# The second feed-forward layer by seven half-size products a slice

## The chip, the cores and the metric

The kernel runs on one core of a Trainium2 chip. The metric is the device time of one execution in microseconds. Before the change it is 1483.28 us, the median of 3 runs (1483.11 to 1483.89). A profile of one further execution is read beside it; every row below comes from that execution.

Engines: TensorE (PE: matmuls; PEld: its weight loads), VectorE (DVE), ScalarE (ACT), GpSimd (POOL) and SyncE (SP, which issues loads).

## What is computed

Two transformer blocks over 512 rows of 1024 features, in fp32. The change touches the last part of the second block alone:

```
h = rms_norm_2(x, norm_mlp[l])
x = x + jnp.square(jax.nn.relu(h @ w_ff1[l])) @ w_ff2[l]
return rms_norm_2(x, norm_final)
```

`w_ff1` is 1024 x 4096, `w_ff2` 4096 x 1024. Products have to keep the precision of fp32.

## The kernel before

All engines run programs of their own, ordered by semaphores that are written out by hand. A product in fp32 precision is made of three matmuls: each operand is split into a rounded part ("hi", fp32r) and the remainder ("lo"), and hi x hi, hi x lo and lo x hi are summed in PSUM. A matmul takes a 128x128 block as weights and streams 512 columns.

Weights come as "pairs": 256 rows x 512 columns, two blocks of 128 partitions, 512 KB. SP loads a pair into one of four slots of `raw` (`load`, L514) once TensorE has used the pair that was there (`pair_used`); ScalarE rounds it to `w_hi` (`part_hi`, L1566); GpSimd subtracts and writes `w_lo` (`split`, L677). `w_lo` lies where `raw` lay. TensorE waits for `hi_made` and `lo_made` of each pair.

The feed-forward part works in eight slices of 512 hidden features. The first layer of a slice (`ff_up`, L1519) is a "strip": four pairs, 96 matmuls into four of the eight PSUM banks, features on the partitions. VectorE's `hidden` (L2843) empties it with relu and the row scale and squares it (L2852); ScalarE writes the rounded square `ys_hi` (L2175) and VectorE its remainder `ys_lo` (L2855). The second layer multiplies these 512 rows x 512 features by the slice's 512 x 1024 part of `w_ff2`: two strips of two pairs, 48 matmuls each, rows on the partitions, and VectorE adds each strip from PSUM to x (`add_strip`, L2686), which is kept in `proj[:, :, XRES:XRES+1024]`.

TensorE's order is skewed by one slice: in `ff_step` (L1538) the first layer of slice t+1 comes ahead of the second layer of slice t. VectorE, ScalarE and GpSimd follow in the same order, SP in the order of pairs. The very last strip (`last_strip`, L1522) is done row tile by row tile, so that the final norm of one tile runs beside the matmuls of the next. Ahead of the first slice x is turned (transposed) in TensorE and split into `xt_hi` and `xt_lo`; `r_rows`, the row scale, is spread and turned beside the first strip. `gfin` is the final gain, scaled by one VectorE instruction (L2866) after the first `hidden`.

## Time and profile before

| | us |
|---|---|
| median of 3 runs | 1483.28 |
| lowest, highest | 1483.11, 1483.89 |
| span of the profiled execution | 1481.3 |
| TensorE busy | 1446.9 (98%) |
| VectorE busy | 653.3 (44%) |
| ScalarE busy | 620.0 (42%) |
| GpSimd busy | 651.7 (44%) |

The span goes from the first to the last instruction of the profiled execution. Matmuls overlap in a pipeline, so a busy TensorE may still have matmuls further apart than they could be; the distance between their starts says more than their duration. The feed-forward part fills the span from about 1124 us on. A row's idle time is that of the engine just before the instruction, and the name behind the arrow is what ended it. Idle time of an engine that nobody waits for costs nothing.

### The profile page before, as it was taken

To read this page: it belongs to the slowest core of one execution; us is meant where nothing else is said; L and a number is where in the kernel's file an instruction comes from. 1 tells how busy PE (TensorE), PEld (TensorE's weight loads), DVE (VectorE), ACT (ScalarE), POOL (GpSimd) and SP (SyncE) were. 2 spreads that over 40 slices of the span, in tenths; PEclk is the share of its full clock that TensorE was granted. 3 is DMA by queue.
4 is the path that set the end of the run, shared out by engine and by line. 5 is a ranking of instruction groups with operands and counts; after the bars stand their busy time and mean duration, and the time that the engine had idled before them with its cause. 6 is when DMAs were issued, how large, how long until landed. Compare 5 with 4: busy or idle time off the path is not lost.

```text
span 1481.3 us, 20850 instructions
## 1 busy us (share of the span) xinstructions
PE 1446.9 (98%) x7825; PEld 1212.5 (82%) x7825; DVE 653.3 (44%) x1388; ACT 620.0 (42%) x1128; POOL 651.7 (44%) x451
## 2 busy tenths in 40 slices
PE   8999999989989999999999999999999999999998
PEld 7888888768778888899997777888888888888886
DVE  4436959456563131421244777752222422233233
ACT  5443644567563222343235477762324222222223
POOL 4433645344443444434342365644444444444442
PEclk9999999999999999999999999999999999999999
DMA  6222433203002332446432200004222222223222
GB/s 204 81 81 82 153 94 92 61 7 100 29 1 72 100 93 93 156 126 194 128 89 72 72 16 2 2 13 163 96 100 86 100 100 95 90 99 99 99 96 89
DMA packets 73050, 130.44 MB, mean 88 GB/s; under 512 B 5816, under 2 KB 29955, under 8 KB 72963
## 3 DMA queue, kind: packets, MB, share of 16 engines
q1 hardware_dynamic: 71682, 126.04, 26.8%
q10 hardware_dynamic: 1280, 3.22, 0.6%
q8 instruction: 57, 0.93, 0.3%
q14 instruction: 31, 0.25, 0.1%
HBM read 125.05 MB, written 4.19 MB: 87 GB/s over the span
## 4 chain that ended last, share of the span: by engine, by line
PE 94%; DVE 2%; ACT 2%; issue 1%; POOL 1%; DMA 0%; POOLq 0%; SPq 0%; DVEq 0%; ACTq 0%
PE bank L887 74%; PE bank L1118 4%; PE bank L1126 4%; PE bank L949 3%; PE bank L816 3%; PE bank L847 1%; PE bank L951 1%; PE bank L1534 1%; PE bank L1362 0%; PE bank L1069 0%; DVE prob_t L2496 0%; DMA proj<-in_x 0%; DVE q_parts L2380 0%; POOL w_lo L680 0%; PE bank L1015 0%
## 5 line engine op out<-in xcount | busy, mean ns | idle before, releaser
L680 POOL TENSOR_TENSOR w_lo<-raw,w_hi 128x1024 fp32r<-128x1024 f32 (+3 forms) x217 | 508.0, 2343 | 671.2 <-ACT w_hi L1569 671.1
L1569 ACT ACTIVATE w_hi<-raw 128x1024 fp32r<-128x1024 f32 (+3 forms) x221 | 225.6, 1022 | 610.0 <-DMA raw<-in_w_ff 254.6
L887 PE MATMUL bank<-w_hi,xt_hi 128*128 128x484 f32 (+2 forms) x632 | 236.0, 373 | 0.0
L887 PE MATMUL bank<-w_hi,xt_lo 128*128 128x484 f32 (+2 forms) x632 | 233.8, 370 | 0.0
L887 PE MATMUL bank<-w_lo,xt_hi 128*128 128x484 f32 (+2 forms) x632 | 233.7, 370 | 0.0
L887 PE MATMUL bank<-xt_hi,w_hi 128*128 128x512 f32 x560 | 221.2, 395 | 0.0
L887 PE MATMUL bank<-xt_hi,w_lo 128*128 128x512 f32 x560 | 218.2, 390 | 0.0
L887 PE MATMUL bank<-xt_lo,w_hi 128*128 128x512 f32 x560 | 218.0, 389 | 0.0
L887 PEld LDWEIGHTS bank<-w_hi,xt_lo 128*128 128x128 f32 x632 | 118.6, 188 | 14.6
L887 PEld LDWEIGHTS bank<-w_hi,xt_hi 128*128 128x128 f32 x632 | 118.7, 188 | 14.5 <-issue 0.4
L887 PEld LDWEIGHTS bank<-w_lo,xt_hi 128*128 128x128 f32 x632 | 118.7, 188 | 13.8
L887 PEld LDWEIGHTS bank<-xt_hi,w_hi 128*128 128x128 f32 x560 | 105.2, 188 | 23.3 <-issue 2.2
L887 PEld LDWEIGHTS bank<-xt_hi,w_lo 128*128 128x128 f32 x560 | 105.1, 188 | 22.1
L887 PEld LDWEIGHTS bank<-xt_lo,w_hi 128*128 128x128 f32 x560 | 105.2, 188 | 21.5 <-issue 0.5
L887 PE MATMUL bank<-w_hi,ys_hi 128*128 128x512 f32 x240 | 93.4, 389 | 0.0
L887 PE MATMUL bank<-w_lo,ys_hi 128*128 128x512 f32 x240 | 93.4, 389 | 0.0
L887 PE MATMUL bank<-w_hi,ys_lo 128*128 128x512 f32 x240 | 93.4, 389 | 0.0
L2849 DVE SCALAR_TENSOR_TENSOR proj<-bank,r_rows 128x512 f32<-128x512 f32 x32 | 19.9, 683 | 140.3 <-PE bank L887 140.3
L1833 ACT ACTIVATE sc<-sc,negmax 128x512 f32<-128x512 f32 (+3 forms) x104 | 58.8, 567 | 24.7 <-DVE negmax L2472 24.7
L2691 DVE TENSOR_TENSOR proj<-proj,bank 128x512 f32<-128x512 f32 x56 | 34.7, 682 | 69.4 <-PE bank L887 69.4
L816 PE MATMUL bank<-cst,proj 128*128 128x128 f32 (+2 forms) x368 | 50.6, 280 | 7.7 <-DMA proj<-in_x 4.9
L816 PEld LDWEIGHTS bank<-cst,proj 128*128 128x128 f32 (+2 forms) x368 | 43.6, 141 | 13.8 <-DMA cst<-cst_d 4.1
(386 smaller groups left out, 2383.3 us busy)
## 6 DMA issues: line engine op xcount, KB each, us to landing
raw<-in_w_ff SPq DMA_DIRECT2D x64, 512.0 KB, 3.5
raw<-in_w_in SPq DMA_DIRECT2D x40, 512.0 KB, 3.5
raw<-in_w_in SPq DMA_DIRECT2D x40, 484.0 KB, 3.4
raw<-in_w_in SPq DMA_DIRECT2D x24, 392.0 KB, 3.3
raw<-in_w_out SPq DMA_DIRECT2D x16, 512.0 KB, 3.5
raw<-in_w_branch SPq DMA_DIRECT2D x12, 512.0 KB, 3.7
raw<-in_w_mem_kv SPq DMA_DIRECT2D x8, 512.0 KB, 3.6
raw<-in_w_proj_nsa SPq DMA_DIRECT2D x8, 512.0 KB, 3.4
```

Of the source, the lines that this page charges most:

```text
L680: pool.tensor_tensor(w_lo[:, slot, 0:halves, 0:width], raw[:, slot, 0:halves, 0:width], w_hi[:, slot, 0:halves, 0:width].bitcast(F32), ALU ...
L816: ins = pe.transpose(b[0:m, o:o + k], src, ident[0:k, 0:k])
L847: ins = pe.matmul(bank[strip_banks(s)][b][:], lhs, rhs, start=False, stop=kk == 1 and j == 2)
L887: ins = pe.matmul(o, lhs, rhs, start=st and j == 0, stop=en and j == 2)
L949: ins = pe.matmul(o, w["q"], w["k"], start=True, stop=w["k_lo"] is None)
L951: ins = pe.matmul(o, w["q"], w["k_lo"], start=False, stop=True)
L1118: ins = pe.transpose(bank[TURN_BANK + u % 2][0:n, t * P:(t + 1) * P], src[:, t * P:t * P + n], ident)
L1126: ins = pe.matmul(bank[4 + w["pas"] % 2][w["rows"], w["cols"]], w["v"][t], src[0:n, t * P:(t + 1) * P], start=w["start"] and t == 0, stop= ...
L1569: act.activation(w_hi[:, slot, 0:halves, 0:width], raw[:, slot, 0:halves, 0:width], ACT.Copy)\
L1833: act.activation(v, v, ACT.Exp, scale=-1.0, bias=negmax[:, u % SC:u % SC + 1], accum_out=sums[:, u % SC:u % SC + 1]).then_inc(sem["exps"], 1)
L2691: ins = dve.tensor_tensor(v, v, banks[t][:], ALU.add)
L2849: ins = dve.scalar_tensor_tensor(relu[:, m, :], banks[m][:], 0.0, r_rows[:], ALU.max, ALU.mult)
```

## The change

Seven of the eight slices take another algorithm for the second layer; the first layer stays. The slice's activations (512 x 512) are seen as 2 x 2 quarters a11, a12, a21, a22 of 256 x 256, and the slice's weights as 2 x 2 quarters b11, b12, b21, b22 of 256 x 512. Four sums of a-quarters and four differences of b-quarters (one of them in place of b12) are made, and seven products of 256 x 256 by 256 x 512 are summed to give what eight gave.

- TensorE: `product` is 2 x 2 x 3 = 12 matmuls into two banks; `seven_products` orders them 6, 1, 7, 5, 4, 2, 3. It waits for all three `h_hi` and `h_lo` of the slice ahead of the first, for the item (`item_hi`, `item_lo`) ahead of each, and for banks emptied by VectorE. The next slice's strip waits until six of the seven products are added.
- VectorE: four half sums (512 columns for each partition), four quarter sums or differences (1024), three remainders of rows (`rows_lo`: 1024, 512, 2048), then `hidden` of the next slice, then adding the seven products from PSUM, with the square between the third and the fourth. Products 2, 3, 4, 5 go to one quarter of x each; 1, 6 and 7 are kept in `part_sums` and joined to x by five instructions of 1024 columns after the seventh slice.
- ScalarE: `rows_hi` (1024, 512, 2048 columns) and `items_hi` (seven of 1024), then the four pairs of the first layer.
- GpSimd: `items_lo` (seven of 1024), then the four `w_lo` of the first layer. Before it had eight `w_lo` a slice.
- SP: the quarters don't pass the ring of four slots; each has its place and is loaded when the product that reads it last is done. Ahead of the first of them SP waits for all of `xt_hi` and `xt_lo`, as they lie where earlier data lay, and it loads them ahead of the second strip's pairs.
- The eighth slice keeps two strips. Its parts lie in the place of `xt_hi` and `xt_lo`, and its remainder is made after the seventh slice's last product is added.

The core of the diff:

```diff
+PRODUCTS = (6, 1, 7, 5, 4, 2, 3)
+ITEMS = (1, 6, 7, 5, 4, 2, 3)
+ITEM_AFTER = {1: 1, 6: 4, 7: 2, 5: 3, 4: 4, 2: 4, 3: 3}
+RAW_FREE = {"b11": 1, "b12": 7, "b21": 2, "b22": 3}
...
+            def ff2_quarters(f):
+                for n, (name, q, s) in enumerate((("b11", 0, 0), ("b12", 0, 1), ("b21", 1, 0), ("b22", 1, 1))):
+                    if not isinstance(f, int):
+                        sp.wait_ge(sem["product_done"], f * 7 + (PRODUCTS.index(RAW_FREE[name]) - 6))
+                    src = pairs_of(w_ff2_2[0], 0, 0)[f * 2 + q]
+                    sp.dma_start(quarter[name][:], src[:, :, S * s:S * s + S]).then_inc(sem[f"quarter_in{n}"], 16)
...
             ff1_weights(0, PAIR_FF)
-            with sp.Fori(1, 8) as f:
-                ff1_weights(f, f * 8 + (PAIR_FF - 4))
-                ff2_weights(f - 1, f * 8 + PAIR_FF)
-            ff2_weights(7, PAIR_FF + 60)
+            sp.wait_ge(sem["xt_hi"], 24)
+            sp.wait_ge(sem["xt_lo"], 24)
+            ff2_quarters(0)
+            ff1_weights(1, PAIR_FF + 4)
+            with sp.Fori(1, 7) as f:
+                ff1_weights(f + 1, f * 4 + (PAIR_FF + 4))
+                ff2_quarters(f)
...
+            def items_lo(i, t):
+                for n, m in enumerate(ITEMS):
+                    pool.wait_ge(sem["item_hi"], at(i, lambda j: 7 * t(j) + n + 1))
+                    pool.wait_ge(sem["t_made"], at(i, lambda j: 4 * t(j) + ITEM_AFTER[m]))
+                    pool.tensor_tensor(item_lo[m][:], quarter[item_of[m]][:], item_hi[m][:].bitcast(F32), ALU.subtract)\
+                        .then_inc(sem["item_lo"], 1)
...
+            ff1_lo(0, lambda j: PAIR_FF + 4)
+            items_lo(0, lambda j: 0)
+            ff1_lo(0, lambda j: PAIR_FF + 8)
+            with pool.Fori(1, 7) as i:
+                items_lo(i, lambda j: j)
+                ff1_lo(i, lambda j: PAIR_FF + 8 + 4 * j)
...
+            def product(m, banks, first):
+                (a_hi, a_lo), b_hi, b_lo = rows_of[m], item_hi[m], item_lo[m]
+                for kt in range(2):
+                    for u in range(2):
+                        c = slice(u * P, u * P + P)
+                        for j, (lhs, rhs) in enumerate(((a_hi[:, kt, c], b_hi[:, kt, :]), (a_hi[:, kt, c], b_lo[:, kt, :]),
+                                                        (a_lo[:, kt, c], b_hi[:, kt, :]))):
+                            ins = pe.matmul(bank[banks + u][:], lhs, rhs, start=first and kt == 0 and j == 0,
+                                            stop=kt == 1 and j == 2, skip_group_check=True)
+                ins.then_inc(sem["product_done"], 1)
+            def seven_products(i, parity, t):
+                def taken(n):
+                    pe.wait_ge(sem["product_added"], at(i, lambda j: 7 * t(j) + n))
+                pe.wait_ge(sem["h_hi"], at(i, lambda j: 3 * t(j) + 3))
+                pe.wait_ge(sem["h_lo"], at(i, lambda j: 3 * t(j) + 3))
+                two, one, three = 4 * parity, 4 * parity + 2, 4 - 4 * parity
+                for m in PRODUCTS:
+                    n = ITEMS.index(m)
+                    pe.wait_ge(sem["item_hi"], at(i, lambda j: 7 * t(j) + n + 1))
+                    pe.wait_ge(sem["item_lo"], at(i, lambda j: 7 * t(j) + n + 1))
+                    if m == 6:
+                        if not isinstance(i, int):
+                            taken(0)
+                        product(6, two, True)
+                    elif m == 1:
+                        product(1, one, True)
+                    elif m == 7:
+                        taken(1)
+                        product(7, two, False)
+                    elif m == 5:
+                        pe.wait_ge(sem["emptied_d"], at(i, lambda j: strips_emptied("D", STRIP_FF + 1 + t(j))))
+                        product(5, three, True)
+                    elif m == 4:
+                        taken(3)
+                        product(4, two, False)
+                    elif m == 2:
+                        taken(2)
+                        product(2, one, False)
+                    else:
+                        taken(4)
+                        product(3, three, False)
...
+            pe.wait_ge(sem["h_hi"], 22)
+            pe.wait_ge(sem["h_lo"], 22)
+            pe.wait_ge(sem["product_added"], 48)
+            strip(0, lambda j: STRIP_LAST, lambda j: PAIR_LAST, 2, h_last, S, False)
+            pe.wait_ge(sem["product_added"], 49)
+            last_strip(STRIP_LAST + 1, PAIR_LAST + 2)
...
+            def rows_hi(i, t):
+                act.wait_ge(sem["sq_out"], at(i, lambda j: t(j) + 1))
+                if not isinstance(i, int):
+                    act.wait_ge(sem["product_done"], at(i, lambda j: 7 * t(j)))
+                act.activation(a1_hi[:], h_raw[:, :, 0:256], ACT.Copy).then_inc(sem["h_hi"], 1)
+                act.activation(a22_hi[:], h_raw[:, 2:4, 256:512], ACT.Copy).then_inc(sem["h_hi"], 1)
+                act.wait_ge(sem["h_summed"], at(i, lambda j: t(j) + 1))
+                act.activation(s_hi[:], h_sums[:], ACT.Copy).then_inc(sem["h_hi"], 1)
+            def items_hi(i, t):
+                for m in ITEMS:
+                    name = item_of[m]
+                    if name in ("b11", "b21", "b22"):
+                        act.wait_ge(sem[{"b11": "quarter_in0", "b21": "quarter_in2", "b22": "quarter_in3"}[name]],
+                                    at(i, lambda j: 16 * t(j) + 16))
+                    else:
+                        act.wait_ge(sem["t_made"], at(i, lambda j: 4 * t(j) + ("t1", "b12", "t2", "t4").index(name) + 1))
+                    act.activation(item_hi[m][:], quarter[name][:], ACT.Copy).then_inc(sem["item_hi"], 1)
+            def ff_step(i, t):
+                rows_hi(i, t)
+                items_hi(i, t)
+                his(i, lambda j: PAIR_FF + 8 + 4 * t(j))
...
+            act.wait_ge(sem["sq_out"], 8)
+            act.wait_ge(sem["pair_used"], PAIR_LAST)
+            act.activation(h_last[0], h_raw, ACT.Copy).then_inc(sem["h_hi"], 1)
...
+            def hidden(i, f):
+                banks = strip_wait(i, lambda j: STRIP_FF + f(j))
+                wait(dve, sem["h_hi"], at(i, lambda j: 3 * f(j)))
+                wait(dve, sem["h_lo"], at(i, lambda j: 3 * f(j)))
                 for m in range(4):
-                    ins = dve.scalar_tensor_tensor(relu[:, m, :], banks[m][:], 0.0, r_rows[:], ALU.max, ALU.mult)
+                    ins = dve.scalar_tensor_tensor(h_raw[:, m, :], banks[m][:], 0.0, r_rows[:], ALU.max, ALU.mult)
                 ins.then_inc(sem["emptied_d"], 1)
-                dve.wait_ge(sem["emptied_d"], at(i, lambda j: strips_emptied("D", s(j))))
-                dve.tensor_tensor(square, relu, relu, ALU.mult).then_inc(sem["sq_out"], 1)
-                dve.wait_ge(sem["sq_out"], at(i, lambda j: f(j) + 1))
-                dve.wait_ge(sem["h_hi"], at(i, lambda j: f(j) + 1))
-                dve.tensor_tensor(ys[parity][1][:], square, ys[parity][0][:].bitcast(F32), ALU.subtract)\
-                   .then_inc(sem["h_lo"], 1)
+            def square(i, f):
+                dve.wait_ge(sem["emptied_d"], at(i, lambda j: strips_emptied("D", STRIP_FF + f(j))))
+                dve.tensor_tensor(h_raw, h_raw, h_raw, ALU.mult).then_inc(sem["sq_out"], 1)
+            def rows_lo(i, t):
+                dve.wait_ge(sem["h_hi"], at(i, lambda j: 3 * t(j) + 1))
+                dve.tensor_tensor(a1_lo[:], h_raw[:, :, 0:256], a1_hi[:].bitcast(F32), ALU.subtract).then_inc(sem["h_lo"], 1)
+                dve.wait_ge(sem["h_hi"], at(i, lambda j: 3 * t(j) + 2))
+                dve.tensor_tensor(a22_lo[:], a22, a22_hi[:].bitcast(F32), ALU.subtract).then_inc(sem["h_lo"], 1)
+                dve.wait_ge(sem["h_hi"], at(i, lambda j: 3 * t(j) + 3))
+                dve.tensor_tensor(s_lo[:], h_sums[:], s_hi[:].bitcast(F32), ALU.subtract).then_inc(sem["h_lo"], 1)
+            def add_product(i, t, m, banks):
+                dve.wait_ge(sem["product_done"], at(i, lambda j: 7 * t(j) + PRODUCTS.index(m) + 1))
+                for u in range(2):
+                    o = {2: proj[:, u, XRES:XRES + S], 3: proj[:, u, XRES + S:XRES + D],
+                         4: proj[:, 2 + u, XRES:XRES + S], 5: proj[:, 2 + u, XRES + S:XRES + D]}.get(m)
+                    z = {1: 0, 6: 1, 7: 2}.get(m)
+                    if o is not None:
+                        ins = dve.tensor_tensor(o, o, bank[banks + u][:], ALU.add)
+                    elif isinstance(i, int):
+                        ins = dve.tensor_copy(part_sums[z][:, u, :], bank[banks + u][:])
+                    else:
+                        ins = dve.tensor_tensor(part_sums[z][:, u, :], part_sums[z][:, u, :], bank[banks + u][:], ALU.add)
+                ins.then_inc(sem["product_added"], 1)
...
+                t1, t2, t4 = quarter["t1"][:], quarter["t2"][:], quarter["t4"][:]
+                b11, b12, b21, b22 = (quarter[n][:] for n in ("b11", "b12", "b21", "b22"))
+                if not isinstance(i, int):
+                    dve.wait_ge(sem["product_done"], at(i, lambda j: 7 * t(j)))
+                dve.wait_ge(sem["sq_out"], at(i, lambda j: t(j) + 1))
+                dve.tensor_tensor(h_sums[:, 2], a11, a21, ALU.subtract)
+                step_(i, t, 0, dve.tensor_tensor(h_sums[:, 0], a21, a22, ALU.add))
+                step_(i, t, 1, dve.tensor_tensor(h_sums[:, 1], h_sums[:, 0], a11, ALU.subtract))
+                dve.tensor_tensor(h_sums[:, 3], a12, h_sums[:, 1], ALU.subtract).then_inc(sem["h_summed"], 1)
+                dve.wait_ge(sem["quarter_in0"], at(i, lambda j: 16 * t(j) + 16))
+                dve.wait_ge(sem["quarter_in1"], at(i, lambda j: 16 * t(j) + 16))
+                dve.tensor_tensor(t1, b12, b11, ALU.subtract).then_inc(sem["t_made"], 1)
+                dve.wait_ge(sem["quarter_in3"], at(i, lambda j: 16 * t(j) + 16))
+                dve.wait_ge(sem["t_made"], at(i, lambda j: 4 * t(j) + 1))
+                dve.tensor_tensor(b12, b22, b12, ALU.subtract).then_inc(sem["t_made"], 1)
+                dve.tensor_tensor(t2, b22, t1, ALU.subtract).then_inc(sem["t_made"], 1)
+                dve.wait_ge(sem["quarter_in2"], at(i, lambda j: 16 * t(j) + 16))
+                dve.wait_ge(sem["t_made"], at(i, lambda j: 4 * t(j) + 3))
+                dve.tensor_tensor(t4, b21, t2, ALU.subtract).then_inc(sem["t_made"], 1)
+                rows_lo(i, t)
+                two, one, three = 4 * parity, 4 * parity + 2, 4 - 4 * parity
+                hidden(i, lambda j: t(j) + 1)
+                add_product(i, t, 6, two)
+                add_product(i, t, 1, one)
+                add_product(i, t, 7, two)
+                square(i, lambda j: t(j) + 1)
+                add_product(i, t, 5, three)
+                add_product(i, t, 4, two)
+                add_product(i, t, 2, one)
+                add_product(i, t, 3, three)
+            def step_(i, t, n, ins):
+                ins.then_inc(sem["half_sums"], 1)
+                dve.wait_ge(sem["half_sums"], at(i, lambda j: 2 * t(j) + n + 1))
             dve.wait_ge(sem["r_kept"], 1)
-            hidden(0, 0, lambda j: STRIP_FF, lambda j: 0)
+            hidden(0, lambda j: 0)
...
+            dve.wait_ge(sem["h_hi"], 22)
+            dve.tensor_tensor(h_last[1], h_raw, h_last[0].bitcast(F32), ALU.subtract).then_inc(sem["h_lo"], 1)
+            dve.wait_ge(sem["product_added"], 49)
+            upper, lower = proj[:, 0:2, XRES:XRES + D], proj[:, 2:4, XRES:XRES + D]
+            for v, z in ((upper[:, :, S:D], 0), (lower[:, :, 0:S], 0), (lower[:, :, S:D], 0)):
+                ins = dve.tensor_tensor(v, v, part_sums[z][:], ALU.add)
+            ins.then_inc(sem["sums_joined"], 1)
+            dve.wait_ge(sem["sums_joined"], 1)
+            for v, z in ((upper[:, :, S:D], 1), (lower[:, :, S:D], 2)):
+                ins = dve.tensor_tensor(v, v, part_sums[z][:], ALU.add)
+            ins.then_inc(sem["sums_joined"], 1)
+            dve.wait_ge(sem["sums_joined"], 2)
+            residual(2, STRIP_LAST, 0)
```

## Rows read from the trace of the kernel before

**Rows 1.** Page: span, then each engine's busy us, share, instructions.

```profile
span 1481.3 us, 20850 instructions
...
PE 1446.9 (98%) x7825; PEld 1212.5 (82%) x7825; DVE 653.3 (44%) x1388; ACT 620.0 (42%) x1128; POOL 651.7 (44%) x451
```

**Rows 2.** Chain that ended last, from 1100: start us, us, what.

```profile
1145.28 318.29 PE bank L887 x1404
```

**Rows 3.** Groups by line, 1050:1482: busy us, mean ns of one | idle before, releaser.

```profile
L680 POOL TENSOR_TENSOR w_lo<-raw,w_hi 128x1024 fp32r<-128x1024 f32 x75 | 180.8, 2411 | 229.8 <-ACT w_hi L1569 229.8
...
L1569 ACT ACTIVATE w_hi<-raw 128x1024 fp32r<-128x1024 f32 x75 | 79.6, 1061 | 297.1 <-DMA raw<-in_w_ff 254.6 <-DMA raw<-in_w_out 29.5 <-DMA raw<-in_w_proj_nsa 13.1
...
L2852 DVE TENSOR_TENSOR proj<-proj 128x2048 f32<-128x2048 f32 x8 | 18.3, 2292 | 0.3
...
L2175 ACT ACTIVATE ys_hi<-proj 128x2048 fp32r<-128x2048 f32 x8 | 15.2, 1903 | 0.0
```

**Rows 4.** VectorE, then GpSimd, in one slice: start us, us, instruction [idle before <-releaser].

```profile
1307.02 2.78 DVE L2855 TENSOR_TENSOR ys_lo<-proj,ys_hi 128x2048 fp32r<-128x2048 f32 x1 [1.64 <-ACT ys_hi L2175]
...
1322.16 2.48 DVE L2691 TENSOR_TENSOR proj<-proj,bank 128x512 f32<-128x512 f32 x4 [8.40 <-PE bank L887]
...
1305.18 2.46 POOL L680 TENSOR_TENSOR w_lo<-raw,w_hi 128x1024 fp32r<-128x1024 f32 x1 [3.08 <-ACT w_hi L1569]
...
1321.56 2.41 POOL L680 TENSOR_TENSOR w_lo<-raw,w_hi 128x1024 fp32r<-128x1024 f32 x1 [3.13 <-ACT w_hi L1569]
```

**Rows 5.** VectorE, then GpSimd, at 764:785.

```profile
764.62 0.69 DVE L2281 TENSOR_TENSOR rot_q<-proj,cst 128x512 f32<-128x512 f32 x1
765.22 0.69 DVE L2282 TENSOR_TENSOR rot_q<-proj,cst 128x512 f32<-128x512 f32 x1
765.94 0.69 DVE L2283 TENSOR_TENSOR proj<-rot_q 128x512 f32<-128x512 f32 x1
...
767.27 2.87 DVE L2279 TENSOR_TENSOR rot_q<-proj,cst 128x512 f32<-128x512 f32 x1
...
767.22 2.37 POOL L680 TENSOR_TENSOR w_lo<-raw,w_hi 128x1024 fp32r<-128x1024 f32 x1 [4.28 <-ACT w_hi L1569]
```

**Rows 6.** VectorE, then GpSimd, at 226:236.

```profile
226.01 4.43 DVE L2241 TENSOR_TENSOR proj<-proj,rstd 128x4096 f32<-128x4096 f32 x1
230.47 2.39 DVE L2259 TENSOR_TENSOR junk<-proj,gained_a 128x256 f32<-128x256 f32 x1
232.78 2.50 DVE L2260 TENSOR_TENSOR junk<-proj,gained_a 128x256 f32<-128x256 f32 x1
...
227.38 7.62 POOL L680 TENSOR_TENSOR w_lo<-raw,w_hi 128x968 fp32r<-128x968 f32 x2 [2.29 <-ACT w_hi L1569]
```

**Rows 7.** VectorE, then ScalarE, where the feed-forward layers begin, 1085:1195.

```profile
1134.24 1.41 DVE L2269 SCALAR_TENSOR_TENSOR xt_lo<-bank,vec,xt_hi 128x512 fp32r<-128x512 f32 x2 [1.13 <-ACT xt_hi L1598]
...
1157.32 0.68 DVE L2866 TENSOR_SCALAR gfin<-gfin 128x1024 f32<-128x1024 f32 x1
...
1145.31 0.60 ACT L2163 ACTIVATE r_rows<-bank 128x512 f32<-128x512 f32 x1 [4.12 <-PE bank L816]
```

**Rows 8.** Page: queue, MB, share; loads, KB, us to landing; then windows with GB/s.

```profile
q1 hardware_dynamic: 71682, 126.04, 26.8%
...
raw<-in_w_ff SPq DMA_DIRECT2D x64, 512.0 KB, 3.5
...
10.00:12.00 2.00, 2.00 (x6) 1.66 (x5) 1.36 (x2) 1.40 (x2) 1.92 (x3) 1.00 1.05 405
```

**Rows 9.** Windows (PE busy first, PEclk, DMA share, GB/s), then TensorE's first matmuls.

```profile
1474.00:1476.00 2.00, 0.45 (x2) 0.02 (x1) 1.58 (x5) 1.06 (x5) 0.54 (x1) 1.00 0.68 262
1479.00:1480.00 1.00, 0.00 (x0) 0.00 (x0) 0.00 (x0) 0.00 (x0) 0.00 (x0) 0.86 0.99 381
...
9.10 1.95 PE L1069 MATMUL bank<-w_hi,xt_hi 128*128 128x484 f32 x4
...
12.25 1.03 PE L1069 MATMUL bank<-w_hi,xt_hi 128*128 128x484 f32 x4
```

92 lines of the change are left out of this document (45 added, 47 removed).

## Prediction, made before the change was run

> **What bounds the kernel now.** I read the page's busy shares first, then the chain that ended last, then the groups of the feed-forward stretch. TensorE is busy for 1446.9 of 1481.3 us [rows 1]. From 1145.28 us the chain is TensorE alone: 1404 matmuls in 318.29 us, 0.2267 us each, without a gap at any strip, wait or loop turn [rows 2]. So in this stage a matmul less is worth 0.2267 us, as long as nothing else ends later. The other engines have slack: in one slice of 192 matmuls (43.5 us) GpSimd makes eight w_lo of 2.40 us, 19 us in all [rows 3].
>
> The reader should then look at how VectorE and GpSimd meet. A VectorE instruction with both inputs in SBUF and 512 columns takes 0.69 us alone and 2.87 us when it starts 0.05 us after a w_lo: it ends 0.5 us after the w_lo has ended [rows 5]. A slice of the feed-forward shows the same in small: a ys_lo that starts 0.6 us before a w_lo ends takes 2.78 us, against 2.29 us for a square of the same size [rows 3, 4]. In 226 to 235 us it goes both ways: the w_lo waits for a long VectorE instruction, then they take turns one by one [rows 6]. Adding from PSUM is free of it: 2.48 us for four beside a w_lo that keeps its 2.41 us [rows 4]. So a GpSimd subtraction and a VectorE instruction with two SBUF inputs exclude each other, and the change adds many of both.
>
> A rule speaks against this change here. The Trainium skill, SBUF — State Buffer, "Who interferes with whom", has the first of the two hold the shared ports for its whole instruction while the other "fully blocks". Rows 5 agree, with their 2.87 us. If it did not hold for this change, the sum below would be lower by the 6.6 us of part 3 and the 1.4 us that hang on them.
>
> **Part 1, fewer matmuls.** A slice of the second layer had 2 strips x 2 pairs x 2 x 4 x 3 = 96 matmuls; a product has 2 x 2 x 3 = 12, seven make 84. Shapes are the same (128x128 weights, 512 columns). Seven slices: 84 fewer, x 0.2267 = **-19.0 us**. The waits ahead of each product (two to four) stand where the kernel before has up to five ahead of a strip, at no cost in rows 2. I take nothing for them; bounds are 0 and 0.1 us for each of 49, together 5 us.
>
> **Part 2, the steady slice.** 96 + 84 = 180 matmuls, 40.8 us. I set T = 0 at the end of a slice's last product. PE then does the next first-layer strip (96 matmuls) and wants the parts of the rows and the first items at 21.6. What has to be late for that, by instruction: VectorE adds the last product (two from PSUM, half of 2.48 us [rows 4]) until 1.3; four half sums of 512 columns, 0.6 us each with 0.1 for the two that wait for VectorE's own result [rows 5], until 4.1; three differences of 1024 columns (half of 2.29, about 1.1 each [rows 3]) until 7.6. The fourth quarter's load goes out at 0 and lands at 3.5 [rows 8], ahead of its use at 5.3. ScalarE meanwhile rounds: rows by 1.6, sums (2048 columns, 1.9 us) from 4.2 to 6.1, the first item (1.06 us) by 7.1 [rows 3]. Here GpSimd begins its seven items and the turns start: item until 9.9, fourth difference until 11.1, the first row remainder, which needs nothing new, 12.2, item 14.5, second remainder 15.1, item 17.4, last remainder (2048 columns) 19.6. That is 2 us ahead of PE. If no turn were lost it would be 12.6; one turn more, 22.0, a stall of 0.4 us.
>
> GpSimd has eleven subtractions now, 26.4 us; VectorE's instructions with two SBUF inputs are 2.4 + 4.5 + 3.9 + 2.2 (square) = 13.0 us. Together 39.4 of 40.8 us. The items are needed from 21.6 on, one each 2.7 us, and the last is made by 29; the four w_lo that follow end at about 40.5, needed from 40.8 on. VectorE's adds (1.3 us for a product that takes 2.7) leave about 1.3 us at each point where PE waits for an emptied bank; the square sits between the third and fourth and waits one turn, still in time. So I count **0 us** for a steady slice, and note that it is 97% full.
>
> **Part 3, the first slice.** Here the chain starts later. SP used to load the second strip's pairs as slots came free; now it waits for the turned x, whose last part is made at 1135.65 [rows 7], and puts four quarters ahead of them. A load alone lands 3.5 us after its issue and loads in a row move at 405 GB/s, 1.3 us for 512 KB [rows 8]: quarters land from 1139.3 to 1143.2, the first pair at 1144.5; with 1.06 and 2.40 us [rows 3] its w_lo is ready at 1148.1, where PE wants it at 1147.8: **+0.3 us** (0 to 1.7: 126.04 MB in 26.8% of the span [rows 8] make 1.65 us for each of the five loads). r_rows, made at 1145.3 before [rows 7], comes two roundings later, still ahead of 1148.2. Then VectorE empties the strip until 1150.7 and finds GpSimd in the second strip's w_lo: square from 1152.7 to 1155.0, w_lo until 1157.3, gfin (0.68 us [rows 7]) until 1158, half sums until 1160.9, differences until 1164.4, item, difference, remainder, item, remainder, item, last remainder until 1176.4. PE has finished its strip at 1169.9. **+6.6 us**. Without any blocking this chain ends at 1165.3 and costs nothing; with one more turn it costs 9.
>
> After 6.6 us of idling TensorE's clock may be lower. At the kernel's end the last matmul ends at 1474.45 and the granted clock falls to 0.50 (1.2 of 2.4 GHz) at about 1479.7, 5.3 us later; the first matmuls of all take 0.44 us each, and 0.22 from 12.25 us on [rows 9]. The eight between 9.10 and 12.25 took 3.15 us in place of 1.75: **+1.4 us** (0 to 3).
>
> **Part 4, the end.** The eighth slice keeps the old form, but its lower part h_lo is now made after the last add: add until 1.3, subtraction of 2048 columns until 3.6, while PE could start at -0.2: **+3.8 us** (3.7 to 6, if a w_lo is still running). That is shorter than 5.3 us, so no clock falls. Joining the sums (five of 1024 columns, some 6 us on VectorE) lies beside the next strip's 48 matmuls, 10.9 us: nothing. If that cover were gone it would be the full 6. The bytes loaded are the same.
>
> **Sum.** -19.0 + 0.3 + 6.6 + 1.4 + 3.8 = -6.9 us. The profiled execution spans 1481.3, so 1474.4 after; the median stands 2.0 us over that span, which gives 1483.3 - 6.9 = **1476.4 us**.
>
> **Rivals.** *Clean*: the instructions fall so that few turns are lost in the first slice. For it: one turn is all a VectorE instruction loses, and some of the w_lo may be done early. Against it: rows 5, and GpSimd has three w_lo waiting just there. Then -19.0 + 3.8 + 0.3 = -14.9, **1468.4**.
>
> *One turn more*: GpSimd gets in between the fourth difference and the first remainder in each slice. Then 0.4 to 1.1 us in each of six: 2.4 to 6.6, **1479 to 1483**. It speaks for it that GpSimd's wait ends just as VectorE's instruction does; against it that VectorE's next needs no new event.
>
> *The shared port as the bound* (the other side): GpSimd's w_lo run past the next slice's T by more than 1.3 us, so half sums and differences also lose turns, each 2.35 us. It decides from a ready point of 22.8, where six slices lose the 6.9 us; two turns beyond my 19.6 make 24.3, a stall of 2.7 in six slices, 16 us: **1492.6**, slower. For it: 39.4 of 40.8 us, with nothing for gaps. Against: a stall lengthens the slice and frees the port.
>
> *It doesn't save what it says*: waits ahead of short products cost up to 5 us: 1481.
>
> **How the numbers follow.** Forecast 0.57 (own range 1473 to 1480), clean 0.11, one turn more or costly waits 0.20, port bound 0.12. The range takes in clean and one turn more and reaches toward the port bound: 1468 to 1486. A measurement of this kernel tells about 0.2%, 3.0 us, from no change. Faster by more (under 1480.3): 0.55 of the forecast, all of clean, half of one turn more: 0.76. Within (1480.3 to 1486.2): 0.02 + 0.10 + 0.02: 0.14. Slower: the port bound: 0.10.
>
> **What would show it.** Matmuls 7741 by count in place of 7825, and 40.8 us from slice to slice in the steady part. In the first slice an idle PE of 6 to 7 us just ahead of the first product, released by VectorE's s_lo; at the end one of 3.8 us, released by h_lo. VectorE's 1024-column differences at a mean well over 1.2 us, the surplus being GpSimd's. A gap ahead of the first product of each steady slice would speak for one turn more, and gaps of over 2 us with w_lo past the slice's end for the port. I am wrong if the order of turns is another than rows 6 show, or if the waits inside the products cost PE time.

## The result, and the profile after

The changed kernel takes **1498.54 us** (median of 4 runs, 1497.79 to 1500.97) against 1483.19 of the kernel before in the same comparison: ratio 1.0104, 95% interval 1.009 to 1.0119. It is slower by 15.3 us; 6.9 us faster was forecast, and 1486 was the upper end of the range. The time is above even the "shared port as the bound" rival (1492.6). The profiled execution spans 1496.1 us, against 1481.3 in [rows 1].

The page of the changed kernel, first the span and the engines, then groups (busy us, mean ns of one, idle time before and its releaser):

```profile
span 1496.1 us, 21004 instructions
...
PE 1440.0 (96%) x7741; PEld 1202.2 (80%) x7741; DVE 822.3 (55%) x1505; ACT 648.9 (43%) x1163; POOL 735.7 (49%) x472
...
L824 POOL TENSOR_TENSOR item_lo<-quarter_b,item_hi 128x1024 fp32r<-128x1024 f32 x28 | 73.1, 2625 | 73.9 <-ACT item_hi L2292 73.9
L824 POOL TENSOR_TENSOR item_lo<-quarter_t,item_hi 128x1024 fp32r<-128x1024 f32 x21 | 71.0, 3397 | 8.2 <-DVE quarter_t L3018 8.2
...
L1603 PE MATMUL bank<-item_hi,s_hi 128*128 128x512 f32 x112 | 46.6, 416 | 15.0 <-DVE proj L2991 9.6
```

The 84 matmuls are gone (7741 in place of 7825). Against [rows 2], where 1404 matmuls follow each other without a gap, the products now have 15 us of idle time ahead of them, 9.6 of it put down to VectorE's adds of line 2991. TensorE's waits from 1120 us on (us in all, times, longest) say where:

```profile
PE bank L1603 <- DVE proj L2991: 9.6, 3, 3.3
PE bank L1603 <- DVE s_lo L2981: 5.4, 1, 5.4
PE bank L944 <- issue: 3.6, 1, 3.6
PE bank L944 <- POOL w_lo L718: 1.5, 1, 1.5
```

The chain that ended last gives the length of each slice (start us, us, what; L944 is the first layer's strip, L1603 the products):

```profile
1179.06 21.10 PE bank L1603 x84
1200.16 21.79 PE bank L944 x96
1221.94 8.31 PE bank L1603 x36
...
1241.73 3.02 PE bank L1603 x12
1244.75 21.80 PE bank L944 x96
1266.56 19.41 PE bank L1603 x84
1285.96 21.78 PE bank L944 x96
...
1462.07 3.63 issue
1465.70 12.66 PE bank L944 x48
```

From one end of a slice's products to the next (T to T) the six steady slices take 44.6 (1200.16 to 1244.75), 41.2, 45.8, 41.6, 47.1 and 41.6 us. Every second one is long, and each long one stops ahead of its last product. VectorE around that stop, in the first slice that is long and in the second that is not, then GpSimd in both (start us, us):

```profile
1230.28 1.29 DVE L2995 TENSOR_TENSOR part_sum<-part_sum,bank 128x512 f32<-128x512 f32 x2 [1.46 <-PE bank L1603]
1231.48 8.91 DVE L2972 TENSOR_TENSOR proj<-proj 128x2048 f32<-128x2048 f32 x1
1240.32 3.66 DVE L2991 TENSOR_TENSOR proj<-proj,bank 128x512 f32<-128x512 f32 x6
...
1276.10 4.16 DVE L2972 TENSOR_TENSOR proj<-proj 128x2048 f32<-128x2048 f32 x1
1280.18 2.47 DVE L2991 TENSOR_TENSOR proj<-proj,bank 128x512 f32<-128x512 f32 x4
```

```profile
1228.76 9.49 POOL L718 TENSOR_TENSOR w_lo<-raw,w_hi 128x1024 fp32r<-128x1024 f32 x4
...
1273.32 11.58 POOL L718 TENSOR_TENSOR w_lo<-raw,w_hi 128x1024 fp32r<-128x1024 f32 x4
```

Line 2972 is the square. At 1231.48 it is asked for during the second of four queued w_lo and runs only when all four are done: the four take 9.49 us together, undisturbed, and the square ends at 1240.4. Behind it stand the adds of products 5 and 4, and product 3 waits for those. At 1276.10 the same square loses one turn (4.16 us), and now the four w_lo take 11.58 us. Six squares of the steady slices: 8.91, 4.16, 8.91, 3.81, 9.01, 3.81 us.

The difference of the two spans, +14.8 us, piece by piece: -19.0 (84 matmuls); +2.2 before the layers begin (x is turned at 1131.57 in place of 1129.42; in the sixteen kernels below, which change nothing ahead of this point, it lies between 1129.01 and 1130.81, and in the one that repeats the changed kernel at 1130.23, so most of the 2.2 is not the change's); +0.3 and +1.5 for the second strip's w_lo; +5.4 ahead of the first product; +2.1 on the first slice's 84 matmuls (21.10 in place of 19.04); +17.0 in the six steady slices; +3.6 and +1.8 at the end. The 17.0 are three stops (9.6), a product's matmuls at 0.2311 us in place of 0.2267 (19.41 us for 84, 2.2 in six slices), and slower matmuls after the stops. The granted clock fell after the second and the third stop and not after the first; after the second it reads:

```profile
1329.00:1331.00 2.00, 2.00 (x6) 1.60 (x5) 0.79 (x2) 0.00 (x0) 0.00 (x0) 0.50 0.00 0
```

(PE, PEld, DVE, ACT, POOL busy, then the granted clock in the third place from the end, DMA share, GB/s.)

### The profile page after: what moved, and what is told of

It is laid out like the page before. It is cut to its first block, busy times and chain, and to the rows that moved or that the text cites. A ratio compares the mean times of both kernels' runs of the same rounds, so it can differ in the third digit from the quotient of the medians.

```text
span 1496.1 us, 21004 instructions
## 1 busy us (share of the span) xinstructions
PE 1440.0 (96%) x7741; PEld 1202.2 (80%) x7741; DVE 822.3 (55%) x1505; ACT 648.9 (43%) x1163; POOL 735.7 (49%) x472
## 4 chain that ended last, share of the span: by engine, by line
PE 88%; DVE 4%; issue 3%; ACT 2%; DMA 1%; POOL 1%; SPq 0%; POOLq 0%; DVEq 0%; ACTq 0%
PE bank L944 61%; PE bank L1603 8%; PE bank L1175 4%; PE bank L1183 4%; PE bank L1006 3%; PE bank L873 3%; PE bank L904 1%; PE bank L1008 1%; DMA raw<-in_w_ff 1%; PE bank L1591 1%; PE bank L1126 0%; DVE proj L2972 0%; DMA proj<-in_x 0%; PE bank L1419 0%; DVE prob_t L2613 0%
## 5 line engine op out<-in xcount | busy, mean ns | idle before, releaser
L718 POOL TENSOR_TENSOR w_lo<-raw,w_hi 128x1024 fp32r<-128x1024 f32 (+3 forms) x189 | 450.1, 2392 | 503.8 <-ACT w_hi L1672 503.7
L1672 ACT ACTIVATE w_hi<-raw 128x1024 fp32r<-128x1024 f32 (+3 forms) x193 | 195.2, 1016 | 439.0 <-DMA raw<-in_w_in 212.0
L944 PE MATMUL bank<-w_hi,xt_hi 128*128 128x484 f32 (+2 forms) x648 | 243.1, 375 | 3.6 <-issue 3.6
L944 PE MATMUL bank<-w_hi,xt_lo 128*128 128x484 f32 (+2 forms) x648 | 240.5, 371 | 0.0
L944 PE MATMUL bank<-w_lo,xt_hi 128*128 128x484 f32 (+2 forms) x648 | 240.5, 371 | 0.0
L944 PE MATMUL bank<-xt_hi,w_hi 128*128 128x512 f32 x560 | 221.8, 396 | 1.5 <-POOL w_lo L718 1.5
L944 PE MATMUL bank<-xt_lo,w_hi 128*128 128x512 f32 x560 | 218.5, 390 | 0.0
L944 PE MATMUL bank<-xt_hi,w_lo 128*128 128x512 f32 x560 | 218.3, 390 | 0.0
L944 PEld LDWEIGHTS bank<-w_hi,xt_hi 128*128 128x128 f32 x648 | 122.1, 188 | 19.2 <-issue 4.4
L944 PEld LDWEIGHTS bank<-w_hi,xt_lo 128*128 128x128 f32 x648 | 122.0, 188 | 15.4
L944 PEld LDWEIGHTS bank<-w_lo,xt_hi 128*128 128x128 f32 x648 | 122.2, 189 | 14.6
L944 PEld LDWEIGHTS bank<-xt_hi,w_hi 128*128 128x128 f32 x560 | 105.5, 188 | 25.4 <-issue 2.2
L944 PEld LDWEIGHTS bank<-xt_hi,w_lo 128*128 128x128 f32 x560 | 105.4, 188 | 22.4
L944 PEld LDWEIGHTS bank<-xt_lo,w_hi 128*128 128x128 f32 x560 | 105.5, 188 | 21.6 <-issue 0.5
L824 POOL TENSOR_TENSOR item_lo<-quarter_b,item_hi 128x1024 fp32r<-128x1024 f32 x28 | 73.1, 2625 | 73.9 <-ACT item_hi L2292 73.9
L824 POOL TENSOR_TENSOR item_lo<-quarter_t,item_hi 128x1024 fp32r<-128x1024 f32 x21 | 71.0, 3397 | 8.2 <-DVE quarter_t L3018 8.2
L1603 PE MATMUL bank<-item_hi,s_hi 128*128 128x512 f32 x112 | 46.6, 416 | 15.0 <-DVE proj L2991 9.6
L2278 ACT ACTIVATE a_hi<-proj 128x1024 fp32r<-128x1024 f32 x7 | 7.4, 1063 | 109.0 <-PE bank L1603 107.9
L763 POOL TENSOR_SCALAR proj<-proj,rsum,gsig 128x512 f32<-128x512 f32 (+3 forms) x64 | 39.2, 623 | 31.2 <-DVE rsum L2604 31.0
```

What stands on the lines that cost most here:

```text
L718: pool.tensor_tensor(w_lo[:, slot, 0:halves, 0:width], raw[:, slot, 0:halves, 0:width], w_hi[:, slot, 0:halves, 0:width].bitcast(F32), ALU ...
L763: pool.tensor_scalar(v, v, rsum[:, u % SC:u % SC + 1], gate, ALU.mult, ALU.mult)\
L824: pool.tensor_tensor(item_lo[m][:], quarter[item_of[m]][:], item_hi[m][:].bitcast(F32), ALU.subtract)\
L944: ins = pe.matmul(o, lhs, rhs, start=st and j == 0, stop=en and j == 2)
L1603: ins = pe.matmul(bank[banks + u][:], lhs, rhs, start=first and kt == 0 and j == 0, stop=kt == 1 and j == 2, skip_group_check=True)
L1672: act.activation(w_hi[:, slot, 0:halves, 0:width], raw[:, slot, 0:halves, 0:width], ACT.Copy)\
```

## The experiments

Theory: the square costs the 17 us, because a VectorE instruction that meets a run of queued w_lo may lose all its turns, not one. Rival: the products' own waits and the fuller slice (39.4 of 40.8 us) are to blame. The first three kernels take the square out of the way in three manners.

**e1_delay**: the square is asked for half a microsecond later.

```
+                dve.memset(v_c[:], 0.0)
                 dve.tensor_tensor(h_raw, h_raw, h_raw, ALU.mult)
```

> The changed kernel with one VectorE memset of 512 columns (0.485 us in its trace) ahead of each square, nothing else. In the changed kernel the square waits for three w_lo in a row in slices 1, 3 and 5 (8.9 to 9.0 us), where it asks 0.34 to 0.37 us after the start of the second w_lo, and for one in slices 2, 4 and 6 (3.8 to 4.2 us), where it asks 0.42 to 0.75 us after it. Theory 'phase': the moment at which the square asks decides; 0.5 us later no square takes over 4.6 us, the three stalls go, and the time falls by 14 to 17 us to about 1483. Theory 'queue': whatever finds queued w_lo waits for all of them by chance of something else; the times of the squares stay mixed and the time stays within 3 us of 1498. Theory 'loop half': slices 1, 3 and 5 are the first half of the unrolled loop body and something of that half is at fault; their squares stay at 8.4 us or more and the time stays at 1498 to 1500.

1480.28 us (one run). All six squares take 3.62 us, and every steady slice 41.2 us (21.79 + 19.41). The square's row (minimum, median, maximum ns of the eight), then TensorE's waits:

```profile
L2973 DVE TENSOR_TENSOR proj<-proj x8: 2228/3619/3628, 1152.3 to 1436.6; 128x2048 f32<-128x2048 f32 x8
```

```profile
PE bank L1603 <- issue: 3.9, 1, 3.9
PE bank L944 <- issue: 3.6, 1, 3.6
PE bank L944 <- POOL w_lo L718: 2.2, 1, 2.2
```

The stops of line 2991 are gone with 18 us of time, though nothing was made cheaper. A full slice is not the cause. The stop ahead of the second strip is 2.2 us here, and after it the granted clock is 0.50 for 3.4 us, so that this strip's 96 matmuls take 23.62 us in place of 21.79:

```profile
1152.00:1154.00 2.00, 2.00 (x6) 1.59 (x5) 2.00 (x2) 0.91 (x1) 2.00 (x2) 0.50 0.00 0
```

**e2_square_act**: ScalarE squares, after its last rounding of the slice; VectorE's square goes.

```
-                dve.tensor_tensor(h_raw, h_raw, h_raw, ALU.mult).then_inc(sem["sq_out"], 1)
+                act.activation(h_raw, h_raw, ACT.Square).then_inc(sem["sq_out"], 1)
```

> The square is made by ScalarE (1.9 us, after the slice's w_hi) in place of VectorE, so that no VectorE instruction with two SBUF inputs comes while GpSimd makes its w_lo. My account of the changed kernel is 17 us of loss in the steady slices by the square (three stalls of 3.2 us, the lower clock after them, late adds). If it is right: steady slices of 40.8 to 41.3 us, no PE idle in them, and a time of 1480 to 1483; the first slice loses 2 to 3 us less as well. Rival: another VectorE instruction (a difference or a remainder) meets a run of GpSimd subtractions in the same way and the time stays above 1488.

1480.59 us (10 runs), ratio 0.9982 [0.9972, 0.9991]; steady slices 41.2 us, no stop in any. The first of them:

```profile
1195.90 21.78 PE bank L944 x96
1217.69 19.41 PE bank L1603 x84
```

With the square off VectorE the change is worth 2.6 us.

**e3_own_wait**: each w_lo first waits for the end of the one before.

```
+                    pool.wait_ge(sem["lo_made"], at(i, lambda j: p0(j) + q))
                     split(at(i, lambda j: p0(j) + q), (PAIR_FF + q) % RING, 2, S)
```

> The changed kernel, but each of the four w_lo of a slice waits for the end of the one before it, so that none is queued behind a running one (some 0.1 us each, off the path). Theory 'queue or phase': VectorE gets its turn at the first w_lo that ends: no square over 4.7 us, time about 1482 to 1484. Theory 'loop half': unchanged at 1498 or a little more.

1484.33 us (one run). GpSimd, then VectorE, in the same slice as above:

```profile
1231.36 2.40 POOL L718 TENSOR_TENSOR w_lo<-raw,w_hi 128x1024 fp32r<-128x1024 f32 x1 [0.16 <-POOL w_lo L718]
1233.92 4.26 POOL L718 TENSOR_TENSOR w_lo<-raw,w_hi 128x1024 fp32r<-128x1024 f32 x1 [0.16 <-POOL w_lo L718]
```

```profile
1231.55 4.36 DVE L2973 TENSOR_TENSOR proj<-proj 128x2048 f32<-128x2048 f32 x1
```

A gap of 0.16 us lets the square in after one w_lo, in six of six slices (4.34 to 4.37 us). This points to GpSimd starting its next subtraction without a gap as what keeps the square out. The moment is new too, though: the square asks 0.18 to 0.21 us after a w_lo's start, where no steady slice of a run without the gap has a request. Among those runs (table below) the early requests lose most often, which speaks against the moment as the reason here, but it was not tried by itself.

**e4_square_late** (the square behind the add of product 5) and **e5_two_waits** (a second wait, long since satisfied, ahead of each w_lo) ask what opens the way.

```
-                square(i, lambda j: t(j) + 1)
                 add_product(i, t, 5, three)
+                square(i, lambda j: t(j) + 1)
```

> The square comes after the adding of product 5 in place of before it, so that product 3, which waits for that add, doesn't wait for the square. If the loss is the square's wait on the path of product 3, the stalls inside the products go; the adds of products 4 and 2 come after the square and the next strip waits for them: with squares that lose three turns some 2 us a slice are left (1488 to 1494), with squares that lose one, nothing (1481 to 1484).

1490.3 us (one run); squares 6.15, 5.42, 3.04, 6.12, 3.07, 6.15 us: four of six lose every w_lo that is left (two here). One asked for 1.49 us after a w_lo's start loses, one at 1.50 wins. The stops ahead of product 3 are gone, as expected; where the square loses, TensorE stops ahead of the next strip instead (4.6 us in three slices), and 5.0 us ahead of the last slice.

```
+                    pool.wait_ge(sem["xt_lo"], 24)
                     split(at(i, lambda j: p0(j) + q), (PAIR_FF + q) % RING, 2, S)
```

> The changed kernel with one more wait, long satisfied, ahead of each of the slice's four w_lo; so they have two, as the seven items have. In every trace so far a VectorE remainder that meets a running item with the next item queued loses one turn (all of them), while a square that meets w_lo queued one behind the other loses one turn or all that are left (in the changed kernel 3 of 6, with the late square 4 of 6, with the short delay none of 6). Theory 'the wait opens the gap': with two waits no square loses more than one turn, none over 4.6 us, time about 1482. Theory 'it hangs on the moment alone': the extra wait is nothing; some squares still take 6 us or more, or the pattern of losing slices changes without order. Theory 'items and w_lo differ otherwise': as the changed kernel, slices 1, 3, 5 at 8.9 us, 1498.

("The short delay" is that of e1_delay.) 1506.85 us (one run); five of six squares lose all (8.6 to 8.9 us), five stops, 15.4 us. A satisfied wait changes nothing for the better; the time differs from the changed kernel's with the number of squares lost.

**e10_again** is the changed kernel once more, **e11_short_delay** fills 256 columns ahead of the square in place of 512.

> The changed kernel once more, unchanged. If the moment at which the square is asked for decides and the loop makes the phase, the same three squares (slices 1, 3, 5) take 8.9 to 9.0 us and the other three 3.8 to 4.2; 1497.8 to 1499. If it is chance within each execution, the pattern is another, between none and six of six, and the time moves by 3.5 to 4.5 us for each.

1503.61 us (one run). Four squares are lost now (slices 1, 2, 3 and 5), with four stops of 12.5 us:

```profile
L2972 DVE TENSOR_TENSOR proj<-proj x8: 2406/6688/8910, 1152.0 to 1457.9; 128x2048 f32<-128x2048 f32 x8
```

The same kernel loses other squares in another execution. That gives it a spread of its own: 1497.8 to 1503.6 over five executions, where the kernel before stays within 2.9 us in all comparisons (1482.25 to 1485.13).

> Half the delay of e1_delay: a fill of 256 columns (some 0.27 us) ahead of each square, which is then asked for some 0.65 us after the start of the second w_lo. If only a square asked for in the first 0.4 us of a w_lo loses all turns left, all six take 3.5 to 4.0 us, as in e1_delay, and the time is 1480 to 1481. If the danger goes on until 0.8 us (four of six lost in e4_square_late), three to six of six take 8.6 to 8.9 us and the time is 1490 to 1507. If what matters is that an instruction without input in SBUF stands ahead of the square, whatever its length, none is lost.

1489.7 us (one run). One square of six is lost (8.63 us), asked for 0.66 us after the start of its w_lo; four others asked for at 0.65 to 0.67 lose one turn.

The eight executions in which an instruction of VectorE met queued w_lo without a gap (the changed kernel twice, e1, e4, e5, e11 and, below, e13 and e14; six slices each) give, by the time from the start of the running w_lo to the request:

| asked for after | lost all w_lo left | lost one turn |
|---|---|---|
| 0.30 to 0.41 us | 19 | 4 |
| 0.52 to 0.79 us | 7 | 8 |
| 0.92 to 1.50 us | 1 | 9 |

The moment weighs, and it doesn't decide. Nor does the queue alone: in the first slice of the same eight executions the instruction met queued w_lo too, asked for 0.42 to 2.32 us after a start, and never lost all that were left. In e1 it went ahead at once there (2.23 us, while the w_lo that had started 0.42 us earlier took 4.91).

**e13_subtract, e14_mult_same, e15_mult_items, e16_mult_items2**: is it the square or the queue? Each puts one instruction of 512 columns into e2_square_act, its result unused. e13 and e14 put it where the square stood, e15 ahead of the first row remainder, e16 between the first two remainders, where GpSimd has items queued.

```
+                dve.tensor_tensor(v_c[:].rearrange("p a b -> p (a b)"), gfin[:, 0:512], gfin[:, 512:1024], ALU.subtract)
```

and in the other three

```
+                dve.tensor_tensor(v_c[:].rearrange("p a b -> p (a b)"), gfin[:, 0:512], gfin[:, 0:512], ALU.mult)
```

> On e2_square_act, where VectorE has nothing between the adds of products 7 and 5: a subtraction of two different SBUF inputs of 512 columns into a free place, its result unused, stands where the square stood. If it is the queued w_lo that keep VectorE out, whatever VectorE asks for, some of the six take 2.0 us plus 2.35 for each w_lo left, 7 us or more, and with them the 3 us stalls come back (1484 to 1500). If it is something about the square (in place, both inputs the same, 2048 columns), all six take 2.0 to 2.7 us and the time is 1480 to 1482.

> The same with a multiplication of 512 columns by themselves in that place. Against e13_subtract it tells the kind of operation and the two equal inputs from the queue. If the queue of w_lo decides, it fares as e13_subtract does, one or more of six over 7 us. If the square's own form decides, this one loses all turns and e13_subtract does not.

1487.84 and 1486.81 us (one run each). In each, five of six take 7.3 to 7.4 us. e13's row, and one of them with GpSimd's beside it:

```profile
L3027 DVE TENSOR_TENSOR v_c<-gfin x7: 799/7308/7410, 1185.8 to 1442.1; 128x512 f32<-128x512 f32 x7
```

```profile
1227.00 7.30 DVE L3027 TENSOR_TENSOR v_c<-gfin 128x512 f32<-128x512 f32 x1
```

```profile
1224.28 9.48 POOL L718 TENSOR_TENSOR w_lo<-raw,w_hi 128x1024 fp32r<-128x1024 f32 x4
```

A subtraction worth 0.69 us, with different inputs, is kept out as the square was. So it is not the square's own form; it is meeting these queued w_lo. The stops are shorter (7.9 and 8.0 us in five), as the instruction is.

> The multiplication of e14_mult_same ahead of the first row remainder, where GpSimd's queue holds items in place of w_lo. If items differ from w_lo for any VectorE instruction, it takes one turn (2.0 to 2.9 us) in all seven slices and the remainders follow one turn later, so that the last comes 2.4 us later, at 21.6, about when PE wants it: 1480 to 1484. If a multiplication is kept out by any queue, it takes over 7 us in some slices, the first product waits over 4 us there, and the time is over 1490.

1488.14 us (one run), over the 1480 to 1484 expected. The multiplication began before GpSimd had an item and took 0.68 us, so its own time tells nothing of turns. But it made the first row remainder late, which now met an item, 0.38 to 0.45 us after its start, and took 3.43 us in place of 1.21. So 0.6 us more ahead of the remainders cost a turn on top, and TensorE waits 0.7 us for s_lo in each of six slices (and 6.0 us in the first, for 3.2 in e2).

> In e15_mult_items the multiplication began before GpSimd had an item to do and so never met one. Here it stands between the first and the second row remainder, where an item has just begun and more of them are queued. If a queue of items lets any VectorE instruction in, it takes one turn (2.4 to 2.6 us) in each of the seven slices, and the two remainders behind it one more each; the last is ready some 2.4 us later and the first product waits 2.0 to 2.5 us in each steady slice: 1493 to 1497. If equal inputs or a multiplication are what is kept out, it takes over 7 us in some slices.

1488.81 us (one run), under the 1493 to 1497 expected. VectorE, then GpSimd:

```profile
1211.19 2.90 DVE L2980 TENSOR_TENSOR v_c<-gfin 128x512 f32<-128x512 f32 x1
1214.01 2.89 DVE L2982 TENSOR_TENSOR a_lo<-proj,a_hi 128x512 fp32r<-128x512 f32 x1
1216.83 4.48 DVE L2984 TENSOR_TENSOR s_lo<-h_sums,s_hi 128x2048 fp32r<-128x2048 f32 x1
```

```profile
1210.21 3.33 POOL L824 TENSOR_TENSOR item_lo<-quarter_t,item_hi 128x1024 fp32r<-128x1024 f32 x1 [1.16 <-DVE quarter_t L3021]
1213.50 2.85 POOL L824 TENSOR_TENSOR item_lo<-quarter_b,item_hi 128x1024 fp32r<-128x1024 f32 x1
```

The multiplication takes 2.89 to 2.90 us in seven of seven: one turn. Its cost for TensorE, 0.7 us a slice, was a third of what I expected: the last remainder came 2.8 us later, and 2.5 of those were slack (T + 19.3 to the strip's end at T + 21.8); the rest of the 0.7 is the 0.4 between the remainder's end and the first matmul. By itself this run doesn't set items apart from w_lo: the multiplication asked 0.92 to 0.98 us after an item's start, and at 0.92 to 1.50 us queued w_lo let VectorE in too, nine times of ten. The remainders do. In every changed kernel s_lo asks 0.51 to 0.53 us after the start of an item with another queued behind it, and lost one turn in 117 cases of 117; the first remainder of e15 lost one in seven of seven at 0.38 to 0.45. Queued w_lo kept VectorE out in 7 of 15 and 19 of 23 cases near those moments, though they are the same GpSimd instruction with the same 1024 columns. Why is open. Beside the w_lo ScalarE is idle and VectorE has just added from PSUM; beside the items ScalarE rounds. Neither was tried as a cause.

The Trainium skill, SBUF — State Buffer, "Who interferes with whom", which the prediction drew on, calls the use of the shared ports "an exclusive lock" and has a VectorE instruction with two SBUF inputs contend with a GpSimd instruction that reads SBUF; in that section "fully blocks" stands beside VectorE's 2-port modes. Both queues agree with the lock, turn by turn (2.90 us for 0.68 beside an item, 4.16 for 2.3 beside a w_lo). That the first of the two holds the ports doesn't tell who comes next: in the 27 lost cases w_lo that started 0.9 to 4.4 us after VectorE's request ran ahead of it.

**e6_tail, e7_start, e8_all, e9_first, e12_tail_first** take up the other terms, all on e2_square_act. e6 makes the eighth slice's row remainder ahead of two adds (the upper edit; VectorE's loop leaves its last two slices written out for it); e7 loads two pairs of the second strip ahead of the quarters and moves gfin to the end; e8 is both; e9 and e12 add to e8 and e6 that GpSimd's third item of the first slice waits for the last remainder (the lower edit).

```
                 add_product(i, t, 4, two)
+                if isinstance(i, int) and i == 6:
+                    dve.wait_ge(sem["h_hi"], 22)
+                    dve.tensor_tensor(h_last[1], h_raw, h_last[0].bitcast(F32), ALU.subtract)
                 add_product(i, t, 2, one)
...
                 for n, m in enumerate(ITEMS):
+                    if isinstance(i, int) and n == 2:
+                        pool.wait_ge(sem["h_lo"], 3)
```

> The square on ScalarE as before, and the last slice's remainder moved ahead of the adds of products 2 and 3 of the seventh slice. In the kernel with the square on ScalarE TensorE idles 3.2 us ahead of the last slice and its 48 matmuls then take 13.7 in place of 10.9 us at the lower clock. If both go: 6.0 us less, 1474.6. If the remainder meets the last w_lo and holds the add of product 2 back: up to 1.5 us of idling are left, the clock stays up: 1476. Rival: the slow matmuls there aren't the stall's doing; then they stay at 13.7 and only 3 us are gained: 1477.5.

> The square on ScalarE, and at the start of the layer two pairs of the second strip are loaded ahead of the quarters, gfin is made at the end. My account of the first slice: 1.5 us wait for r_rows, 3.2 us for the last remainder, 2 us by the lower clock after it. With the pairs first the r_rows wait goes (-1.5), without gfin and with the w_lo out of the way the remainder is 1 to 2 us late in place of 3.2, and the clock stays up: 4 to 5 us less than the kernel with the square on ScalarE, 1475.5 to 1476.5. Rival: loading the quarters later makes the differences late and the gain is given back: 1480.

> All three together: square on ScalarE, last remainder ahead of the last adds, pairs before quarters and gfin at the end. If the losses are independent, the gains of the last two add: about 10 us less than with the square on ScalarE alone, 1470 (84 fewer matmuls are worth 19.0 us, products pay 0.37 us a slice more for their own matmuls, 2.6 us, and 2 to 3 us of idling are left). Rival: the start's stall only moves into slice 1: 1474.

> e8_all with one more edit in the first slice: GpSimd makes the third item only once VectorE has made the last row remainder (a wait for h_lo at 3 ahead of it). The mechanism (each GpSimd subtraction queued between two VectorE subtractions costs VectorE one turn of 2.3 us): the last remainder is ready 2.3 us earlier, the stall ahead of the first product is 0.7 to 1.0 us in place of 3.1, and without the long stall the clock stays up, so that the 84 matmuls after it take 19.4 to 19.8 us in place of 22.4. Together 1468.5 to 1469.5 against 1473.3 of e8_all. The rival (the fall of the clock has nothing to do with that stall): the 84 matmuls still take over 21.5 us and the time is 1471 or more. If the third item, now made later, is late itself, PE waits up to 2.4 us ahead of product 7 and nothing is gained.

> The same edit on e6_tail, where the wait for the second strip's w_lo (1.4 us) is left at the start and the 3.2 us stall ahead of the first product did not lower the clock. The mechanism: stall 0.9 in place of 3.2, 1471.9 against 1474.2. If the time goes below 1471, stalls at the start cost more than their own length here too; if it stays at 1474, the third item has become late in place of the remainder.

| kernel | us (runs) | ratio [95%] | ahead of first product | its 84 matmuls | at the end | 48 matmuls |
|---|---|---|---|---|---|---|
| e2 | 1480.59 (10) | 0.9982 [0.9972, 0.9991] | 3.2 | 21.20 | 3.6 | 13.71 |
| e6 | 1474.16 (4) | 0.9937 [0.9921, 0.9954] | 3.2 | 19.64 | 0.5 | 11.13 |
| e7 | 1480.02 (6) | 0.9970 [0.9957, 0.9982] | 3.1 | 22.53 | 3.6 | 13.93 |
| e8 | 1473.32 (4) | 0.9931 [0.9915, 0.9948] | 3.1 | 22.44 | 0.6 | 11.16 |
| e9 | 1468.98 (4) | 0.9905 [0.9888, 0.9921] | 0.9 | 19.66 | 0.5 | 11.16 |
| e12 | 1471.88 (4) | 0.9926 [0.9909, 0.9942] | 1.0 | 19.63 | 0.6 | 11.14 |

The columns from the fourth on are us of the profiled execution. e6, e9 and e12 came out as expected; e7 and e8 missed by 3.3 to 4.5 us. e7 takes the wait ahead of the second strip away (1.5 us in e2) and gains little: the stop ahead of the first product, expected at 1 to 2 us, stays at 3.1, and its 84 matmuls take 1.3 us more (two of its six executions took 1477.5 us, the others 1480.0 to 1480.4). The remainder comes 1.1 us earlier than in e2, and so does the end of TensorE's strip. Both times lie near the rivals named (1480 and 1474), but neither rival occurred: in e7 the differences don't wait for their quarters, and e8 stops in the first slice and not in slice 1. The windows of e8 show where the time goes:

```profile
1170.00:1173.00 3.00, 0.01 (x1) 0.04 (x1) 2.89 (x1) 0.38 (x1) 3.00 (x2) 0.87 0.58 166
1173.00:1175.00 2.00, 2.00 (x5) 1.61 (x6) 1.97 (x4) 1.06 (x1) 2.00 (x1) 0.50 0.06 22
...
1179.00:1181.00 2.00, 2.00 (x10) 1.55 (x10) 0.78 (x2) 0.00 (x0) 2.00 (x2) 0.98 0.00 0
```

After 3.1 us of idling TensorE runs at 0.50 (1.2 of 2.4 GHz) for 6 us, and 84 matmuls take 22.44 us. In e6 a stop of 3.2 us left the clock at 1.00 and they took 19.64. e9 cuts the stop to 0.9 us and the clock stays up:

```profile
1169.39 0.89 issue
1170.28 19.66 PE bank L1609 x84
1189.94 21.78 PE bank L950 x96
```

e9_first beats both kernels: 14.5 us faster than before, 29.6 faster than the change. The rule behind its last edit, each queued item is one turn of 2.3 us for the remainder, held within 0.1 us (3.1 to 0.9, and 3.2 to 1.0).

## Why the prediction was wrong, point by point

**Part 2, the square: this step failed.** "The square sits between the third and fourth and waits one turn, still in time." It lost three turns in slices 1, 3 and 5, and four slices in the repeat. The reading under it came from [rows 6], where two VectorE instructions of 226 to 235 us take turns with w_lo: only two w_lo stand in that run, so it could not show what a third queued one does. The conclusion "exclude each other" was right, the order of turns was one case taken for a rule. The prediction named that as what would make it wrong; the range gave it nothing. The price is 9.6 us of stops and the slower matmuls after them. e1, e2 and e3 each take it away; e1 and e3 do so with all the work, the square included, where it was.

**Part 2, the rest, was right.** The last remainder was put at T + 19.6; it ends at T + 19.3 in all six slices (1219.41 for 1200.16), with the turns as counted. The port-bound rival (half sums and differences losing turns, w_lo past T) did not occur: the half sums of the six steady slices take 0.68 to 0.70 us. The time ended on that rival's side for another reason. That the slice has little room is right too: 0.6 us more ahead of the remainders costs a turn and with it 0.7 us a slice (e15). The row remainders, and an item that one of them meets and outlasts (VectorE, then GpSimd):

```profile
1212.09 2.90 DVE L2979 TENSOR_TENSOR a_lo<-proj,a_hi 128x512 fp32r<-128x512 f32 x1
1214.92 4.49 DVE L2981 TENSOR_TENSOR s_lo<-h_sums,s_hi 128x2048 fp32r<-128x2048 f32 x1
...
1214.41 2.85 POOL L824 TENSOR_TENSOR item_lo<-quarter_b,item_hi 128x1024 fp32r<-128x1024 f32 x1
```

**Part 1** put 0 to 5 us on the waits inside the products and took 0. The matmuls of the products came to 0.2311 us each, 0.37 us for 84 and 2.6 us in seven slices. The surplus is even over a product and not at its waits: 22 matmuls from 1221.78 to 1226.87 are 0.2314 apart. So the size lies within the bound, but the reason given for the bound doesn't hold. What the true one is stays open: no run looked for it.

**Part 3.** The 6.6 us ahead of the first product were 5.4, released by s_lo as said. The second strip's pairs cost 1.8 us (0.3 and a wait of 1.5) in place of 0.3, just past the bound of 1.7. The clock cost 1.7 us (2.1 less the 0.37 above) in place of 1.4. Together 8.9 for 8.3: right, and e9 shows that most of it can be had back. The 1.4 has luck in it: it was sized from the slow matmuls between 9.10 and 12.25 us, and the profile gives a granted clock of 1.00 for 10 to 12 us [rows 8], so the rows don't show these matmuls at the lower clock. (By the prediction's own figures the stop is 1176.4 - 1169.9 = 6.5 us and the pair's w_lo is ready at 1148.0; each is 0.1 off in the text.)

**Part 4.** The stop was 3.6 us for 3.8. "Shorter than 5.3 us, so no clock falls" was wrong: at 1466 to 1468 the granted clock is 0.50, and the 48 matmuls take 12.66 us in place of 10.9.

```profile
1462.00:1465.70 3.70, 0.07 (x2) 0.03 (x1) 3.59 (x4) 0.00 (x0) 0.00 (x0) 0.98 0.00 0
1466.00:1468.00 2.00, 2.00 (x6) 1.52 (x6) 2.00 (x3) 0.00 (x0) 0.00 (x0) 0.50 0.00 0
```

The 5.3 us of [rows 9] were one fall at the kernel's end, and one fall is no lower bound. It is the same fault as with the square.

With the square out of the way the sum would have been near: e1 and e2 stand at 1480.3 and 1480.6 for a forecast of 1476.4. The missing 4 us, in e2: the wait ahead of the second strip (1.5), the products' matmuls (2.6) and the clock at the end (2.8) and in the first slice (0.4 over the 1.4), less the 3.4 by which the stop ahead of the first product was shorter (3.2 for 6.6).

## What to carry to other kernels

Where a new VectorE instruction with two SBUF inputs falls into a run of back-to-back GpSimd subtractions, price it at the whole rest of the run, and ask who waits behind it: squares of nine us in three slices of six cost some 15 of the 19 us that 84 fewer matmuls save. (The estimate is the 17.0 us of the steady slices less 2.2 for the products' own matmuls.) If it can't be moved to ScalarE (e2), a wait of GpSimd for its own last result, 0.16 us, bounded the loss to one turn in six slices of six (e3). And a rule read off a single case of the trace, a turn lost or a time until the clock fell, needs the range of a guess.

## What was not expected of the hardware

- A VectorE instruction meeting queued w_lo lost all of them in 27 of 48 cases, up to 6.7 us over its own 2.3, while VectorE subtractions meeting queued items lost one turn each time. The result changes from one execution to the next of the same kernel (three and four of six).
- The granted clock fell to 0.50 after stops of 3.1 us (e8) and 3.6 us (the changed kernel's end), and stayed at 1.00 after one of 3.2 us (e6; the 84 matmuls behind it took 19.64 us). Of the changed kernel's three stops of 3.2 to 3.3 us two were followed by a fall. Stops of 2.2 us (e1) and 1.9 us (e14), both ahead of the second strip, were followed by one as well, so the length of the stop alone doesn't decide. A fall cost 1.5 to 2.9 us on the matmuls behind it (19.41 or 19.64 for 84 against 21.10 and 22.53; 11.13 for 48 against 12.66, and 14.03 in e11), from a third of the stop (5.4 us) to nearly all of it (3.1 us).
